# Attention block: the turning of the next head's queries and keys is moved two query tiles later

## What is computed

```python
# FoX: every head, blocks of 128 queries
logits = jnp.einsum('bqhd,bshd->bhqs', qb, k).astype(jnp.float32) * scale
bias = cq.transpose(0, 2, 1)[..., :, None] - cum_keys[..., None, :]
logits = jnp.where(causal[None, None], logits + bias, -jnp.inf)
p = jax.nn.softmax(logits, axis=-1).astype(v.dtype)
return jnp.einsum('bhqs,bshd->bqhd', p, v)
# DSA: the same with the 256 keys of the highest indexer score, no bias
# after both: y @ w_out, then (silu(h @ w_gate) * (h @ w_up)) @ w_down
```

## Time and profile before

| | us |
|---|---|
| median of 3 runs | 1603.93 (1602.62 to 1606.51) |
| the profiled execution | 1601.68 |
| its span, first to last instruction | 1600.0 |
| PE busy in the span | 1499.2 (94%) |
| DVE busy | 892.3 (56%) |
| ACT busy | 510.3 (32%) |
| granted clock of PE, mean | 0.974 |

### The profile page before, as it was taken

The page is one execution under the profiler, slowest core; times in us unless marked ns, Lnnn a source line. Parts: engine busy times, 40 slices in busy tenths (PEclk is TensorE's granted clock), DMA queues, the critical chain, the costliest instruction groups (busy, mean ns, idle before and its releaser), DMA issues.

```text
span 1600.0 us, 20785 instructions
## 1 busy us (share of the span) xinstructions
PE 1499.2 (94%) x7735; PEld 1272.8 (80%) x7735; DVE 892.3 (56%) x1577; ACT 510.3 (32%) x1045; POOL 446.3 (28%) x288
## 2 busy tenths in 40 slices
PE   1899899997998998998999999999999999999998
PEld 1888688885898987887788888888888888888886
DVE  5636889994434568645545225536355263552627
ACT  4524356612565666655534110000100000001012
POOL 2331232241111314250101443242332433314310
PEclk8899999998999999998899999999999999999999
DMA  9021123423005353210300121111111211112102
GB/s 375 28 86 60 53 94 105 166 74 105 2 13 170 97 171 116 70 54 27 132 1 27 54 69 50 40 52 51 54 39 39 61 44 52 39 39 66 40 14 105
DMA packets 88228, 117.46 MB, mean 73 GB/s; under 512 B 4988, under 2 KB 63540, under 8 KB 87128
## 3 DMA queue, kind: packets, MB, share of 16 engines
q1 hardware_dynamic: 88152, 116.44, 22.0%
HBM read 99.58 MB, written 16.84 MB: 73 GB/s over the span
## 4 chain that ended last, share of the span: by engine, by line
PE 83%; DVE 9%; ACT 3%; issue 3%; SPq 1%; DMA 1%; DVEq 0%; ACTq 0%
PE PS L1512 21%; PE PS L1514 21%; PE PS L1513 21%; PE PS L1680 7%; PE PS L1650 5%; DVE gul L1470 2%; PE PS L1667 2%; PE PS L1668 2%; PE PS L1666 1%; DVE LP L1318 1%; DVE acc L1024 1%; PE PS L1712 1%; DMA adar<-in_ada_w_dram 1%; DVE marks_c L1161 1%; ACT QT L863 1%
## 5 line engine op out<-in xcount | busy, mean ns | idle before, releaser
L1512 PE MATMUL PS<-yh,wf 128*128 128x512 f32 x704 | 274.1, 389 | 0.0
L1514 PE MATMUL PS<-yh,wf 128*128 128x512 f32 x704 | 273.9, 389 | 0.0
L1513 PE MATMUL PS<-yl,wf 128*128 128x512 f32 x704 | 273.9, 389 | 0.0
L606 POOL CAST wf<-raw 128x1024 fp32r<-128x1024 f32 x66 | 75.6, 1146 | 568.9 <-PE PS L1514 513.6
L1465 DVE TENSOR_TENSOR gf<-PS,sil 128x512 f32<-128x512 f32 x44 | 30.4, 692 | 356.9 <-PE PS L1514 356.1
L608 POOL TENSOR_TENSOR wf<-raw,wf 128x1024 fp32r<-128x1024 f32 x66 | 168.2, 2549 | 5.4
L1512 PEld LDWEIGHTS PS<-yh,wf 128*128 128x128 f32 x704 | 132.2, 188 | 27.7 <-issue 0.3
L1514 PEld LDWEIGHTS PS<-yh,wf 128*128 128x128 f32 x704 | 132.2, 188 | 27.4
L1513 PEld LDWEIGHTS PS<-yl,wf 128*128 128x128 f32 x704 | 132.2, 188 | 27.3
L952 ACT ACTIVATE sil<-PS 128x512 f32<-128x512 f32 x44 | 26.3, 598 | 395.2 <-PE PS L1514 395.2
L1680 PE MATMUL PS<-Vn,PT 128*128 128x64 f32 x1152 | 144.4, 271 | 0.0
(11 more groups left out here) (257 smaller groups left out, 2847.9 us busy)
## 6 DMA issues: line engine op xcount, KB each, us to landing
adar<-in_ada_w_dram SPq DMA_DIRECT2D x32, 512.0 KB, 3.8
raw<-in_w_in_dram SPq DMA_DIRECT2D x24, 512.0 KB, 4.0
qkv_scratch<-stage SPq DMA_DIRECT2D x48, 256.0 KB, 2.0
raw<-in_w_gate_dram SPq DMA_DIRECT2D x22, 512.0 KB, 3.6
raw<-in_w_up_dram SPq DMA_DIRECT2D x22, 512.0 KB, 3.7
raw<-in_w_down_dram SPq DMA_DIRECT2D x22, 512.0 KB, 3.2
ada<-in_ada_w_dram SPq DMA_DIRECT2D x8, 1024.0 KB, 9.9
xs<-in_x_dram SPq DMA_DIRECT2D x8, 512.0 KB, 9.2
```

The costliest lines, as they stand in the source:

```text
L606: pool.tensor_copy(hi, src).then_inc(w_hi, inc)
L1512: pe.matmul(dst, left[0], right[0], start=first, stop=False)
L1513: pe.matmul(dst, left[0], right[1], start=False, stop=False)
L1514: return pe.matmul(dst, left[1], right[0], start=False, stop=last)
```

## The change

The four P parts are turned in the steps with t = 3, 4, 5, 6 of the head before, where they were in those with t = 1, 2, 3, 4. The same shift is made in all four places that have to agree: the plan of the banks, ACT's copies, DVE's `key_lo` (t = 5 and 6 instead of 3 and 4), and PE's program. No instruction is added or removed. The parts of head 0 itself, which are turned ahead of the loop, stay.

```diff
@@ transposes_plan
-        if s < UNITS and 1 <= t <= 4 and hd + 1 < 2 * NH:
-            order.append(("P", hd + 1, t - 1))
+        if s < UNITS and 3 <= t <= 6 and hd + 1 < 2 * NH:
+            order.append(("P", hd + 1, t - 3))
@@ ACT
-                if s < UNITS and 1 <= t <= 4 and hd + 1 < 2 * NH:
-                    evac_group(("P", hd + 1, t - 1))
+                if s < UNITS and 3 <= t <= 6 and hd + 1 < 2 * NH:
+                    evac_group(("P", hd + 1, t - 3))
@@ DVE
-                if t in (3, 4) and hd + 1 < 2 * NH:
-                    key_lo(hd + 1, t - 1)
+                if t in (5, 6) and hd + 1 < 2 * NH:
+                    key_lo(hd + 1, t - 3)
@@ PE
-                if s < UNITS and 1 <= t <= 4 and hd + 1 < 2 * NH:
-                    turn(("P", hd + 1, t - 1))
+                if s < UNITS and 3 <= t <= 6 and hd + 1 < 2 * NH:
+                    turn(("P", hd + 1, t - 3))
```

## The result

The changed kernel takes 1619.45 us (median of 4, 1617.71 to 1621.11) where the kernel before takes 1604.38 (median of 4, 1602.62 to 1606.51): a ratio of 1.0097, 95% interval 1.0082 to 1.0112, or 15.1 us more. The forecast was 1611.4 with a range up to 1619.0. The sign was right; the size was off by a factor of two and the time is just outside the range.

What follows compares the result with a forecast made beforehand. PE sets the pace in the attention; removed waits against a new stall at t = 6, summed head by head, gave +7.5 us, so 1611.4 us on the median of 1603.93, with a range of 1605.5 to 1619.

Steps and rivals of the forecast that it cites:

- the price of the parts now: Attention before the change: the four P parts with their waits cost 3.49 us a DSA head, 2.79 a FoX head.
- What goes: P0 leaves t = 1 with its 0.45 us wait; the waits at t = 4 and 5 go too.
- The chain: From P2 to T(4)b at t = 6: 5.2 us against PE's 3.65; PE stands 1.54 (FoX) or 1.93 (DSA).
- Heads 1 to 3: FoX heads: new stall against removed waits, +0.5 us each, +1.5 together.
- heads 8 and 12: DSA heads: +0.2 us, and with modulation +0.6; +0.8 together.
- Heads 4, 6, 7: Heads with a modulation in DVE's queue before `key_lo` of P3: +0.9 us each, +2.7 together.
- rival (a): New stalls lower PE's clock: +14 us if only heads 9 and 10 fall, about 1649 if 12 do; chance 0.10.
- The windows at 0.50: Sign of being wrong: windows at 0.50 of PE's clock (1.2 GHz) that were not there before.
- Head 10: DSA head with a 0.6 us square also before `key_lo`: +1.2 us.
- Head 11: T(7)b's 1.57 us wait at t = 1 goes, more at t = 0: -2.3 us, between -1.0 and -2.9.
- Heads 5 and 9: Weight-tile wait ends by the transfer's clock, so shorter t = 1 and 2 buy nothing: +4.5 us together.
- Head 14: M group of 4.34 us between P3 and T(4) covers the chain, so no stall: -1.0 us.

Runs made afterwards that it cites:

- alternating order: Kernel before with its P parts at t = 2 to 5, keys and queries in turn (P2, P0, P3, P1): 1583.63 us, ratio 0.9868.
- POOL late: Changed kernel with POOL's `prepare` held back until DVE has read the logits of t = 6: 1617.24 us, ratio 1.0075.
- key_lo late: Changed kernel with DVE's `biased` before `key_lo` of P2 at t = 5: 1602.05 us, ratio 0.9982.
- P3 behind: Changed kernel with P3 turned behind the two groups of T(4) at t = 6, not ahead of them: 1603.76 us, ratio 1.0002.
- one step earlier: Parts in the old order at t = 2 to 5, one step later than in the kernel before: 1600.30 us, ratio 0.9980.

## Why the prediction came out as it did

- **What bounds, and the price of the parts now (3.49 and 2.79): right.** The alternating order shows it: its heads come to 20.29 and 18.25, where the head of before less the waits gives 20.28 and 18.10.
- **What goes: right.** t = 1 at 2.68 and t = 2 at 2.25 in head 12, against 2.7 and 2.25 in the text. Step t = 5 of DSA heads is 2.25, the bare 1.81 and a part of 0.44.
- **The chain: right to 0.02 us.** Heads 1 to 3 +0.54 against +0.5, heads 8 and 12 +0.6 and 0.0 against +0.8 together, head 13 -0.74 against -0.8. Step t = 6 of head 3 at 4.66 against 4.6. It was not the only wait there, though: with P3 turned behind T(4), PE still stood 0.92 us in that step, behind ACT's copy of T(4)a. The prediction does not have this second wait, nor does its sum need it, since the other one is longer.
- **Heads 4, 6, 7: the term was mis-sized, +8.5 instead of +2.7.** The steps that failed are two. "POOL's `prepare` starts two steps later and is wanted two steps later, its wait stays as it is": true of its wait, but its work now ran beside DVE's longest queue. That is 0.35 us a head (2.09 idle against 1.74 in the run with POOL late). And the clock, which the sum left at its full rate and rival (a) gave a chance of 0.10: it fell behind the stall, 1.4 to 1.6 us in each. The windows at 0.50 that the prediction named as a sign of being wrong are these. With POOL out of the way and the clock up, heads 6 and 7 came to the predicted +0.9.
- **Head 10 (+3.1 instead of +1.2)** has the same two causes: its idle time was 4.11 where a stall of some 2.6 was in the sum; POOL accounts for 1.06, the square's 1.74 instead of 0.68, and the clock fell. Against that, t = 0 and t = 5 gave back some 1.2 more than was said: there the kernel before lost 0.5 and 0.7 against its other DSA heads, which the sum leaves out. The list of what lies on DVE between `biased` and `key_lo` was right; the lengths were those of an engine that runs alone.
- **Head 11 (+0.6 instead of -2.3).** The gain at t = 0 and 1 was there, 3.54 to 2.30 and 6.05 to 3.24, 0.3 more than said, and t = 2 took 0.3 more than in the other heads, so up to t = 5 the head came as said. But the idle time at t = 6 was 3.44, where 2.3 were in the sum, with a modulation stretched to 2.33, and the clock fell behind it.
- **Heads 5 and 9 (+2.2 instead of +4.5).** Head 5 came as said in its sum (+2.75), which is partly luck: POOL's 0.35 is in it, and in the second execution of the same kernel it took 1.5 more. Head 9 did not wait for its weight tile at all: its t = 3 takes 1.34 and not 1.75. The loads in front of that tile are issued behind the modulation of t = 3 in head 8, at 582.90 before and at 595.93 now, 13.0 us later, and head 9 itself starts 16.5 us later (589.40 and 605.88). So the tile had 3.4 us more, most of it because that modulation now runs 8.7 us into head 8 and not 11.6. In head 5 the loads follow the last logits of head 4, at 498.10 and 505.41, 1.5 and 1.6 us ahead of the head, and there the wait stayed. I had tied the transfer to the head and had not asked what issues it.
- **Head 14 (-2.6 instead of -1.0).** Here a low clock of before became shorter, 6.8 us from 718.1 against 3.4 from 737.7, and in the second execution it was not there at all (the head took 23.25). Head 0 is within its range.

An account from the tables, as an estimate: 7.5 predicted; for the clock +4.5 at t = 7 of heads 4, 6, 7, +1.85 at t = 7 of heads 10 and 11, and some 0.7 each at their t = 6; for POOL +3.5 (0.35 in four heads, 1.06 and 1.05 in heads 10 and 11); -2.4 for head 9; -1.6 for head 14; -1.2 for the larger gain of head 10 at t = 0 and 5. That is 13.6, where the attention measured 13.8.

The error of judgement was in weighing rival (a). The evidence against it was one idle time, 1.57 us in head 11 at full clock. The evidence for it was one fall behind 3.42 us. The stalls to come were put at 1.5 to 2.6, between the two, in twelve heads, and one row in a place between does not make 0.10 for twelve draws. The Trainium skill's page "TensorE: Matmul & The Clock Gate", section "A second HAM failure mode: psum-queue depth-cycling", which the prediction set aside, bears on what happened: short idle pieces from a cycle of PSUM banks, and a clock that swings. The runs agree with its direction: the changed kernel falls in heads 4, 6, 7, 10 and 11 besides head 5, where the kernel before has that of head 5 alone between 407.5 and 718.1.

**What stays open.** Where 1.37 us was the only long idle time near by (heads 1 to 3 of four profiles), the clock never fell; with 1.74 to 2.16 at t = 6 it fell in some heads and not in others of the same kernel and length (head 4 but not head 6 in the run with POOL late; head 8 at 1.77 in one kernel and not at 2.16 in another). It also fell behind 1.51, behind 1.62 with 0.41 and behind 1.14 with 0.56 and 0.34 a little earlier (key_lo late, P3 behind, one step earlier); in heads 10 and 11 of the changed kernel, with 4.11 and 3.44, it fell both times. But behind 2.52 in head 10 of the kernel with `key_lo` late it did not. What else decides in between, no run shows. Nor is it settled how much of the whole 15.1 us is POOL's, since taking it away brought falls in heads 8 and 9 that were not there.

## What to carry to other kernels

A group that leaves its bank by two engines needs about 2 us (2.04 here); put a step's work between it and whoever wants that bank, and alternate such groups with ones that leave by a single copy: this gave 1.3% where moving all four parts together cost 1%. When an instruction is put into a queue, ask what stands behind it that a third engine is waiting for: one DVE pass of 0.6 us ahead of `biased` was worth 17 us, some 6 by itself and the rest by what came with it. And when a stall is forecast on the engine that bounds, give its clock a chance for each place and not for the whole, and ask of each engine that is released by the moved work what it will now run beside, and which of the two will start first.

## What the hardware did that I had not expected

- DVE's scalar_tensor_tensor and the square on SBUF operands, and POOL's instructions on SBUF, hold each other up, and in the pairs shown the one that starts second pays: behind POOL's cast or subtraction 1.28 becomes 1.62 or 2.33 and 0.68 becomes 1.74; behind the modulation POOL's cast goes from 0.61 to 1.41 and its copy of 1024 columns from 1.04 to 2.04. `key_lo`, one of whose operands is in PSUM, kept its 0.69 beside POOL's copy in head 3, and the copy its 1.04.
- Stalls of 1.1 to 2.2 us were followed by 3.4 us or more at 1.2 GHz in some heads and not in others. A fall cost 1.4 to 1.6 us of a step of 3.16.
- For one program the heads that fell were the same in two executions, but for heads 5 (at t = 6) and 14.
